# Expert loop: down weights in two places of 4 MB, one kernel before and after

## The chip, the cores and the metric

The kernel runs on one core of one Trainium2 chip. The metric is the device time of one execution in microseconds (us). The core has a matrix engine (TensorE, PE in the profile), a vector engine (VectorE, DVE), a scalar engine (ScalarE, ACT), GpSimd (POOL) and SyncE (SP), which issues all transfers here. Each has its own stream of instructions; they meet at semaphores. On chip there is the SBUF (128 partitions) for operands and the PSUM (8 banks) for products.

## The reference, cut to what matters

A block with attention, a linear recurrence and a mixture of experts comes first, then two layers with attention, pooling and a feed-forward part. Everything is float32, for 256 tokens of width 1024. The change lies in the experts:

```python
logits = (hf @ w_router + b_router)
top_vals, top_idx = lax.top_k(logits, TOP_K)      # 4 of 32 experts for each token
gates = jax.nn.softmax(top_vals, axis=-1)
...
def expert_block(args):                           # xb: the tokens of expert e
    xb, e = args
    gu = xb @ w_gu[e] + b_gu[e]                   # w_gu[e]: 1024 x 2048, 8 MB
    gate = jnp.minimum(gu[:, :D_EXPERT], SWIGLU_LIMIT)
    up = jnp.clip(gu[:, D_EXPERT:], -SWIGLU_LIMIT, SWIGLU_LIMIT)
    glu = gate * jax.nn.sigmoid(SWIGLU_ALPHA * gate)
    return ((up + 1.0) * glu) @ w_down[e] + b_down[e]   # w_down[e]: 1024 x 1024, 4 MB
```

The outputs are weighted by the gates and added up for each token.

## The kernel before, in words

**Stages.** The mixer (attention and recurrence) and the router come first, then the loop over the 32 experts, then the two layers. Expert e is written e0 to e31 below. The weights of the next stage are fetched while the one before computes.

**The ring.** Expert weights go through `ring`, 24576 words (96 KB) in each partition, exactly one expert: eight pieces gu0 to gu7 (1 MB each: 128 rows of w_gu, gate and up) and four pieces dn0 to dn3 (1 MB each: 256 rows of w_down). A piece of expert e+1 goes where the same piece of expert e lay. `load_expert` on SyncE issues one transfer (DMA) for each piece in the order gu0 to gu7, dn0 to dn3. It first waits until TensorE has used the piece that lies there: `gu_used`, or `up_full` for gu7, and `dn_used`, or `y_full` for dn3. SyncE works in order, so a piece that has to wait holds back all behind it. Expert 0's pieces are issued when the mixer has used the ring.

**One expert.** By the count of its tokens an expert takes one round (up to 64 tokens), three (up to 160) or four; `by_count` loads the count into a register and branches to a body written out for that number of rounds, on each of TensorE, ScalarE and VectorE. With this data 30 experts take one round and two take three (their third with 32 slots for each half, called few, L1068 and L1082). A round on TensorE: the bias product (L1072), gate and up with the weights as the moving operand (L1085, 32 matmuls, 64 in the trace since a float32 product runs as two), the combine of the round before (L1051), transposes of the gates (L1103), the gather of the next tokens (L1037), transposes of the hidden values (L1121), transposes of the gathered tokens (L1044), and the down product (L1141, 16 matmuls, 32 in the trace). In between VectorE clips and multiplies (L2086 to L2101) and copies the transposed hidden values (L2104), and ScalarE computes the sigmoid (L1608) and empties banks. A weight piece is given free (`gu_used`, `dn_used`) only in an expert's last round.

**Before the loop.** SyncE sends the gate and up biases to memory and fetches them back transposed (`bias_raw`, L674, "the bias transfers"); ScalarE (L1583) and VectorE (L1977) make `bias_pair` of them and raise `bias_ready`. VectorE adds the mixer's product to x (L1986). The fills of the mixer have names; `o3` is the last attention product, `ad2` the last modulation product, `rt` the transposed router logits.

**Places in the SBUF.** `heap` follows the ring. The mixer's tiles and the experts' small tiles are carved from it, one over the other.

## Time and profile before

| | |
|---|---|
| Time, median of 3 executions | 2127.07 us (2123.1 to 2129.1) |
| The profiled execution's own time | 2125.6 us |
| Its span, from the first to the last instruction | 2123.8 us |
| Mean granted TensorE clock | 0.987 of full speed |
| Gate and up products (L1085) | 492.1 us busy, 2176 matmuls |
| Down products (L1141) | 255.1 us busy, 1152 matmuls |
| Moved by DMA | 580.37 MB, mean 273 GB/s |

The profile shows one execution. An engine's busy time is not its share of the path: a busy engine may be waiting work that something else paces. The loop runs from 186 to 1210 us, 32 us for an expert on average. Which transfers and which products pace it must be read from the waits and from the chain of what released what.

### The profile page before, as it was taken

What the parts mean: (1) busy time and instruction counts of PE and PEld (TensorE: products, weight loads), DVE (VectorE), ACT (ScalarE), POOL (GpSimd) and SP (SyncE); (2) the same over time, 40 slices, a digit from 0 to 9 for tenths busy, and PEclk for the clock granted to TensorE, in tenths of its full rate; (3) what the DMA queues carried; (4) which work ended last, traced back from release to release, by engine and by line L of the source; (5) the groups of instructions that cost most, each with busy time, mean ns of one, the idle gap of its engine ahead of it and who ended that gap; (6) DMA issues with size and microseconds to landing.
All of it is one profiled execution on the core that took longest, in us unless ns stands there. A gap on an engine that the chain in (4) does not pass through costs nothing.

```text
span 2123.8 us, 32004 instructions
## 1 busy us (share of the span) xinstructions
PE 2027.8 (95%) x12406; PEld 1301.0 (61%) x12407; DVE 911.2 (43%) x1611; ACT 645.8 (30%) x981; POOL 59.9 (3%) x65
## 2 busy tenths in 40 slices
PE   6999999999999999999999999999999999999999
PEld 4864333433333333332333498979999899799999
DVE  2522122112222112221112356966786548776774
ACT  1422111101111111110111234564554354644653
POOL 0000000000000000000000022000000120000000
PEclk8997999999999999999999999999999999999999
DMA  9785999299999999999769953423665544234563
GB/s 351 272 329 242 396 417 417 118 417 417 419 418 417 417 419 418 417 417 418 294 250 418 372 153 111 156 72 105 199 214 164 157 132 144 98 120 159 172 196 110
DMA packets 222041, 580.37 MB, mean 273 GB/s; under 512 B 23520, under 2 KB 142048, under 8 KB 185984
## 3 DMA queue, kind: packets, MB, share of 16 engines
q1 hardware_dynamic: 221952, 579.09, 71.6%
q8 instruction: 67, 1.10, 0.2%
q14 instruction: 22, 0.18, 0.0%
HBM read 577.74 MB, written 1.31 MB: 273 GB/s over the span
## 4 chain that ended last, share of the span: by engine, by line
PE 70%; DMA 12%; SPq 9%; DVE 4%; ACT 3%; issue 2%; ACTq 0%; DVEq 0%
PE bank L1085 13%; DMA ring<-in_w_gu 9%; PE bank L1141 8%; SPq L685 4%; SPq L687 4%; PE bank L1226 3%; PE bank L1228 3%; PE bank L1227 3%; PE bank L1457 3%; PE bank L1459 3%; PE bank L1458 3%; PE bank L1037 3%; PE bank L1051 3%; PE bank L812 3%; PE bank L882 2%
## 5 line engine op out<-in xcount | busy, mean ns | idle before, releaser
L1085 PE MATMUL bank<-ring,heap 128*64 128x512 f32 x2176 | 492.1, 601 | 31.7 <-DMA ring<-in_w_gu 31.7
L1085 PEld LDWEIGHTS bank<-ring,heap 128*64 128x64 f32 x2176 | 148.3, 137 | 358.5 <-issue 261.8
L2086 DVE TENSOR_SCALAR heap<-bank 128x256 f32<-128x256 f32 (+1 forms) x72 | 26.7, 413 | 726.2 <-PE bank L1085 697.5
L1141 PE MATMUL bank<-ring,heap 128*64 128x512 f32 (+1 forms) x1152 | 255.1, 595 | 0.0
L1226 PE MATMUL bank<-h_hi,w_hi 128*128 128x256 f32 x640 | 185.2, 289 | 2.2 <-DVE w_lo L2172 1.2
L2367 DVE TENSOR_TENSOR w_lo<-ring,w_hi 128x2048 fp32r<-128x2048 f32 (+1 forms) x64 | 142.4, 2226 | 98.8 <-ACT w_hi L1780 98.8
L1608 ACT ACT_TABLE_LOAD x32 | 41.1, 1283 | 472.5 <-DVE heap L2086 470.8
L1457 PE MATMUL bank<-h_hi,w_hi 128*128 128x256 f32 x640 | 181.7, 284 | 2.4 <-DVE w_lo L2367 2.4
L1227 PE MATMUL bank<-h_lo,w_hi 128*128 128x256 f32 x640 | 182.5, 285 | 0.0
L1228 PE MATMUL bank<-h_hi,w_lo 128*128 128x256 f32 x640 | 182.4, 285 | 0.0
L1458 PE MATMUL bank<-h_lo,w_hi 128*128 128x256 f32 x640 | 181.1, 283 | 0.0
L1459 PE MATMUL bank<-h_hi,w_lo 128*128 128x256 f32 x640 | 181.1, 283 | 0.0
L1141 PEld LDWEIGHTS bank<-ring,heap 128*64 128x64 f32 (+1 forms) x1152 | 78.5, 135 | 150.9 <-issue 145.1
L1780 ACT ACTIVATE w_hi<-ring 128x2048 fp32r<-128x2048 f32 (+1 forms) x64 | 119.2, 1862 | 146.0 <-PE bank L1459 85.5
L2172 DVE TENSOR_TENSOR w_lo<-ring,w_hi 128x2048 fp32r<-128x2048 f32 x52 | 119.3, 2296 | 39.7 <-ACT w_hi L1668 39.7
L1226 PEld LDWEIGHTS bank<-h_hi,w_hi 128*128 128x128 f32 x640 | 124.1, 194 | 5.7 <-DVE w_lo L2172 3.5
L1457 PEld LDWEIGHTS bank<-h_hi,w_hi 128*128 128x128 f32 x640 | 122.8, 192 | 2.8 <-DVE w_lo L2367 2.8
L1227 PEld LDWEIGHTS bank<-h_lo,w_hi 128*128 128x128 f32 x640 | 124.2, 194 | 0.1
L1228 PEld LDWEIGHTS bank<-h_hi,w_lo 128*128 128x128 f32 x640 | 124.2, 194 | 0.0
L1458 PEld LDWEIGHTS bank<-h_lo,w_hi 128*128 128x128 f32 x640 | 122.9, 192 | 0.1
L1459 PEld LDWEIGHTS bank<-h_hi,w_lo 128*128 128x128 f32 x640 | 122.8, 192 | 0.0
L1668 ACT ACTIVATE w_hi<-ring 128x2048 fp32r<-128x2048 f32 x52 | 99.2, 1909 | 72.2 <-PE bank L1228 54.7
(350 smaller groups left out, 2993.7 us busy)
## 6 DMA issues: line engine op xcount, KB each, us to landing
ring<-in_w_gu SPq DMA_DIRECT2D x256, 1024.0 KB, 19.2
ring<-in_w_down SPq DMA_DIRECT2D x128, 1024.0 KB, 22.3
ring<-in_ffn_w_up SPq DMA_DIRECT2D x44, 1024.0 KB, 7.7
ring<-in_w_in SPq DMA_DIRECT2D x32, 1024.0 KB, 8.0
ring<-in_w_ada SPq DMA_DIRECT2D x24, 1024.0 KB, 10.8
ring<-in_ffn_w_down SPq DMA_DIRECT2D x16, 1024.0 KB, 5.4
ring<-in_w_out SPq DMA_DIRECT2D x8, 1024.0 KB, 5.0
ring<-in_w_in SPq DMA_DIRECT2D x3, 2048.0 KB, 26.7
```

The costliest lines, as they stand in the source:

```text
L1085: last = mm(psum[g][both[f], :], xgT[:, k % 4, k // 4, :], wt[:, g, :, :, f, :].rearrange("p i c n -> p (i c) n"), start=False, stop=k == ...
L1141: last = mm(psum[2][FEW * f:FEW * f + n, :], hidT[:, o:o + n], wt[:, 512 * f:512 * (f + 1)], start=k == 0, stop=k == DT - 1)
L1226: mm(out, wh, x[0][:, k, :], start=k == 0, stop=False)
L1227: mm(out, wh, x[1][:, k, :], start=False, stop=False)
L1228: last = mm(out, wl, x[0][:, k, :], start=False, stop=k == nk - 1)
L1457: mm(b[:, g, :], wh, h_hi[:, k, :], start=k == 0, stop=False)
L1458: mm(b[:, g, :], wh, h_lo[:, k, :], start=False, stop=False)
L1459: last = mm(b[:, g, :], wl, h_hi[:, k, :], start=False, stop=k == DT - 1)
L1668: f(hi, src, ACT.Copy).then_inc(S["whi"].sem, 1)
L1780: f(hi, src, ACT.Copy).then_inc(S["whi"].sem, 1)
L2172: v.tensor_tensor(lo, src, hi.bitcast(F32), ALU.subtract).then_inc(S["wlo"].sem, 1)
L2367: v.tensor_tensor(lo, src, hi.bitcast(F32), ALU.subtract).then_inc(S["wlo"].sem, 1)
```

## The change

The down weights get two places of 4 MB, chosen by the parity of the expert: place 0 is where they lay in the ring, place 1 lies in the heap, above the first 4672 words. The transfers of dn for expert e+2 are issued where those of expert e+1 were, after the same waits for expert e; those of expert 1 are issued ahead of the loop, after `rt` and `bias_ready`. The small tiles of the experts move up in the heap, some mixer tiles share space, and `b_down` is loaded after `o3`, ahead of the bias transfers. On TensorE the loop over 32 experts becomes 16 times an inner loop over 2, and the down product is written once for each place, under an If on the parity, in every round of every body.

```diff
@@ -52,6 +52,8 @@
 DN_K = UNIT // T
 SPLIT = 2 * DT * T + 4 * UNIT + 2 * FT * T
 STOP = None
+DOWN_AT = 2 * DT * T + 2 * T + 64
+DOWN_GAP = 8192 + DOWN_AT
 LCH = {"dve": 125, "pool": 23}
 ROUNDS = 4
 CLASSES = ((64, 1), (160, 3), (256, 4))
@@ -266,11 +268,13 @@
 
         with nc.sbuf_tensor("ring", [P, RING], F32) as ring, nc.sbuf_tensor("heap", [P, HEAP], F32) as heap:
             pass
+        with nc.sbuf_tensor("below_down", [P, 16384], F32), nc.sbuf_tensor("down", [P, 2 * DOWN_GAP], F32) as down:
+            pass
         sb("layer_ring", [P, LRING])
         h_hi, h_lo = sb("h_hi", [P, DT, T], F32R), sb("h_lo", [P, DT, T], F32R)
         w_hi, w_lo = sb("w_hi", [P, 2, UNIT], F32R), sb("w_lo", [P, 2, UNIT], F32R)
         f_hi, f_lo = sb("f_hi", [P, FT, T], F32R), sb("f_lo", [P, FT, T], F32R)
-        sb("between", [P, 16384 - LRING])
+        sb("between", [P, HEAP - 2 * (32 + 64 * 4 + 32) - 2 * 512 - 2 * FEW - (SPLIT - (RING - LRING))])
         bias_pair = sb("bias_pair", [P, 2, 512], F32R)
         bias_sel = sb("bias_sel", [P, 2, FEW], F32R)
         psum = [ctx.enter_context(nc.psum_tensor(f"bank{b}", [P, 512], F32))[:, :] for b in range(8)]
@@ -361,6 +365,7 @@
         rstd = take(2, T)
         modT = take(48)
         scale1, scale2 = take(8), take(8)
+        w_route = take(DT, NE)
         qT = take(4, T)
         kT = take(2, T)
         vtok = take(TT, P)
@@ -370,17 +375,14 @@
         lru_a, lru_u = take(4, T), take(4, T)
         lru_t = take(4, T)
         decay, decay2 = take(4), take(4)
-        small_done = take(1)
         mod_rows = take(512)
         w_rg = take(2 * 4, 64)
         small = take(64)
         probs = take(NH, 384)
-        pT = take(2, 384)
+        pT = xg.rearrange("p a b -> p (a b)")[:, 0:2 * 384].rearrange("p (a b) -> p a b", a=2)
         stat = take(8, 2, NH)
         attnT = take(4, T)
-        w_route = take(DT, NE)
-        assert take.areas[0][1] <= 19800, take.areas
-        b_down = heap[0:NE, 19800:19800 + D]
+        assert take.areas[0][1] <= 18752, take.areas
         xn = sq
         merged = sq
         flat_probs = probs.rearrange("p a b -> p (a b)")
@@ -429,13 +431,16 @@
         take_e = Carve()
         take_e.areas[0][1] = 2 * DT * T + 2 * T + 64
 
+        down_two = down.rearrange("p (a b) -> p a b", a=2)
+        take_e(8192)
         x_tok = take_e(512)
         xgT = take_e(4, 2, FEW)
         act_g, act_u, act_s = take_e(512), take_e(512), take_e(512)
         hid, hidT, y_sb = take_e(512), take_e(512), take_e(512)
         sgT = take_e(T)
         pick, pickg = take_e(TT, T), take_e(TT, 2 * T)
-        gateT = take_e(T)
+        gateT = act_g[:, 0:T]
+        b_down = heap[0:NE, take_e.areas[0][1] - 4352:take_e.areas[0][1] - 4352 + D]
         expert_end = take_e.areas[0][1]
         router_at = HEAP - TT * 320
         assert expert_end <= router_at, (expert_end, router_at)
@@ -658,7 +663,6 @@
                 sp.dma_start(mix_piece(name), w_out[:, k:k + 4, :]).then_inc(mix_in[name].sem, 16)
             sp.dma_start(w_route, dram["w_router"].rearrange("(k p) n -> p k n", p=P)).then_inc(route_in.sem, 16)
             sp.dma_start(vec2_all[:, :, :], dram["vec2"]).then_inc(route_in.sem, 16)
-            sp.dma_start(b_down, dram["b_down"]).then_inc(route_in.sem, 16)
             for c in range(DT):
                 last_of("xr1" if c < 2 else "xg1" if c < 4 else "v" if c == 4 else "q1")
                 load_ada(1, c)
@@ -668,13 +672,15 @@
                 else:
                     last_of("ad1")
                 load_ada(2, c)
+            last_of("o3")
+            sp.dma_start(b_down, dram["b_down"]).then_inc(route_in.sem, 16)
             sp.wait_ge(bias_sent.sem, 16)
             sp.wait_ge(merged_ready.sem, 1)
             for g in range(4):
                 sp.dma_start(bias_raw[NE * g:NE * (g + 1)].rearrange("e g (c n) -> e (g c) n", n=P),
                              bias_rows.rearrange("e (b f n) -> f e b n", f=2, n=P)[g % 2]).then_inc(bias_in.sem, 16)
 
-            def load_expert(e, free, names):
+            def load_expert(e, free, names, place=0):
                 gu = dram["w_gu"][e].rearrange("(k p) n -> p k n", p=P)
                 dn = dram["w_down"][e].rearrange("(k p) n -> p k n", p=P)
                 for name in names:
@@ -684,7 +690,8 @@
                     if name.startswith("gu"):
                         sp.dma_start(piece(exp_stream, name, 1)[:, 0, :], gu[:, j, :]).then_inc(exp_in[name].sem, 16)
                     else:
-                        sp.dma_start(piece(exp_stream, name, 2), dn[:, 2 * j:2 * j + 2, :]).then_inc(exp_in[name].sem, 16)
+                        to = down_two[:, place, 2 * D * j:2 * D * (j + 1)].rearrange("p (k n) -> p k n", k=2)
+                        sp.dma_start(to, dn[:, 2 * j:2 * j + 2, :]).then_inc(exp_in[name].sem, 16)
 
             def after_mixer(name):
                 lo = exp_stream.at[name]
@@ -701,8 +708,13 @@
 
             exp_names = [name for name, _ in EXPERT]
             load_expert(0, after_mixer, exp_names[0:4] + exp_names[8:12] + exp_names[4:8])
-            with sp.Fori(0, NE - 1) as e:
-                load_expert(e + 1, after_expert(e), exp_names)
+            last_of("rt")
+            load_expert(1, lambda name: (bias_ready.sem, 1), exp_names[8:], 1)
+            with sp.Fori(0, NE // 2 - 1) as i:
+                for q in range(2):
+                    load_expert(2 * i + q + 1, after_expert(2 * i + q), exp_names[0:8])
+                    load_expert(2 * i + q + 2, after_expert(2 * i + q), exp_names[8:], q)
+            load_expert(NE - 1, after_expert(NE - 2), exp_names[0:8])
             if stop == "moe":
                 sp.wait_ge(xin_ready.sem, 8)
                 sp.dma_start(out.rearrange("(k p) t -> p k t", p=P), xT[:, :, :]).then_inc(out_stored.sem, 16)
@@ -1052,7 +1064,7 @@
                                   skip_group_check=True)
                 return last
 
-            def expert(e, rounds):
+            def expert(e, rounds, q):
 
                 for r, at, u in turns(rounds):
                     final = r == rounds - 1
@@ -1128,21 +1140,28 @@
                     turn_gathered().then_inc(xT_full.sem, u)
 
 
-                    for k in range(DT):
-                        if k % 4 == 0:
-                            pe.wait_ge(hidT_ready.sem, hidT_ready.at(2 * at + (k // 4 + 1) * u, e))
-                        if r == 0 and k % 2 == 0:
-                            pe.wait_ge(exp_in[f"dn{k // 2}"].sem, exp_in[f"dn{k // 2}"].at(16, e))
-                        wt = piece(exp_stream, f"dn{k // 2}", 2)[:, k % 2, :]
-                        h, c, f = k // 4, k // 2 % 2, k % 2
-                        o = P * h + FEW * f + FEWER * c if few else P * (2 * h + c) + FEW * f
-                        n = FEWER if few else FEW
-                        for f in range(2):
-                            last = mm(psum[2][FEW * f:FEW * f + n, :], hidT[:, o:o + n], wt[:, 512 * f:512 * (f + 1)],
-                                      start=k == 0, stop=k == DT - 1)
-                        if final and k % 2 and k < DT - 1:
-                            last.then_inc(dn_used.sem, 1)
-                    last.then_inc(y_full.sem, u)
+                    def down_products(place):
+
+                        for k in range(DT):
+                            if k % 4 == 0:
+                                pe.wait_ge(hidT_ready.sem, hidT_ready.at(2 * at + (k // 4 + 1) * u, e))
+                            if r == 0 and k % 2 == 0:
+                                pe.wait_ge(exp_in[f"dn{k // 2}"].sem, exp_in[f"dn{k // 2}"].at(16, e))
+                            wt = down_two[:, place, D * k:D * (k + 1)]
+                            h, c, f = k // 4, k // 2 % 2, k % 2
+                            o = P * h + FEW * f + FEWER * c if few else P * (2 * h + c) + FEW * f
+                            n = FEWER if few else FEW
+                            for f in range(2):
+                                last = mm(psum[2][FEW * f:FEW * f + n, :], hidT[:, o:o + n], wt[:, 512 * f:512 * (f + 1)],
+                                          start=k == 0, stop=k == DT - 1)
+                            if final and k % 2 and k < DT - 1:
+                                last.then_inc(dn_used.sem, 1)
+                        last.then_inc(y_full.sem, u)
+
+                    with pe.If(q <= 0):
+                        down_products(0)
+                    with pe.Else():
+                        down_products(1)
 
             drained_mix("ht3")
             pe.wait_ge(pick_ready.sem, 1)
@@ -1162,8 +1181,9 @@
                    skip_group_check=True)
             pe.wait_ge(slots_ready.sem, 2)
             pe.wait_ge(bias_ready.sem, 1)
-            with pe.Fori(0, NE) as e:
-                by_count(pe, e, expert)
+            with pe.Fori(0, NE // 2) as i:
+                with pe.Fori(0, 2) as q:
+                    by_count(pe, 2 * i + q, lambda e, rounds: expert(e, rounds, q))
             pe.wait_ge(y_ready.sem, y_ready.at(R, NE))
             combine().then_inc(combined.sem, R)
             pe.wait_ge(xT_ready.sem, xT_ready.at(R, NE))
@@ -2069,7 +2089,7 @@
             select_bias(0).then_inc(sel_ready.sem, 1)
             dve.wait_ge(gate_ready.sem, 1)
             select_gates(0).then_inc(pickg_ready.sem, 1)
-            v.tensor_copy(small_done, gsum[:, 0, 0:1]).then_inc(slots_ready.sem, 1)
+            v.tensor_copy(rstd[:, 1, 0:1], gsum[:, 0, 0:1]).then_inc(slots_ready.sem, 1)
 
             def expert(e, rounds):
                 for r, at, u in turns(rounds):
```

## Rows read from the trace of the kernel before

**Rows 1.** The page: an engine's busy time, GB/s in 40 slices of the span, DMA issues.

```profile
PE 2027.8 (95%) x12406; PEld 1301.0 (61%) x12407; DVE 911.2 (43%) x1611; ACT 645.8 (30%) x981; POOL 59.9 (3%) x65
GB/s 351 272 329 242 396 417 417 118 417 417 419 418 417 417 419 418 417 417 418 294 250 418 372 153 111 156 72 105 199 214 164 157 132 144 98 120 159 172 196 110
...
ring<-in_w_gu SPq DMA_DIRECT2D x256, 1024.0 KB, 19.2
```

**Rows 2.** The chain that ended last: start us, us, what.

```profile
301.70 13.88 PE bank L1085 x64
...
328.90 13.88 PE bank L1085 x64
...
651.45 25.06 DMA ring<-in_w_gu
...
711.70 25.05 DMA ring<-in_w_gu
```

**Rows 3.** Windows: busy time of PE, PEld, DVE, ACT, POOL; clock, DMA share, GB/s.

```profile
170.00:187.00 17.00, 14.36 (x34) 7.64 (x36) 4.91 (x20) 1.64 (x4) 0.00 (x0) 0.54 0.01 1
375.50:411.50 36.00, 35.80 (x201) 13.35 (x204) 4.50 (x12) 4.12 (x8) 0.00 (x0) 1.00 0.01 1
...
366.00:383.00 17.00, 16.80 (x88) 6.62 (x84) 3.98 (x10) 2.69 (x6) 0.00 (x0) 1.00 0.56 223
...
660.00:720.00 60.00, 55.38 (x266) 19.23 (x264) 12.32 (x36) 8.38 (x14) 0.00 (x0) 1.00 1.02 418
```

**Rows 4.** SyncE's timeline, 340 to 480.

```profile
411.83 6.35 SPq L685 DMA_DIRECT2D ring<-in_w_gu  x8
```

**Rows 5.** Timeline, TensorE: e6's first gate and up, e27's last eight.

```profile
356.04 13.95 PE L1085 MATMUL bank<-ring,heap 128*64 128x512 f32 x64
...
1037.99 1.94 PE L1085 MATMUL bank<-ring,heap 128*64 128x512 f32 x8 [0.55 <-DMA ring<-in_w_gu]
```

**Rows 6.** The longest waits from 436 to 1026: total, times, longest.

```profile
PEld bank L1085 <- DMA ring<-in_w_gu: 88.6, 74, 1.5
...
PE bank L1085 <- DMA ring<-in_w_gu: 29.6, 58, 0.6
```

**Rows 7.** Timeline before the loop, 85 to 170.

```profile
116.35 6.77 SPq L674 DMA_DIRECT2D heap<-bias_rows  x4
...
127.66 0.38 PE L949 MATMUL bank<-heap 128*64 128x128 f32 x2
...
137.67 1.05 ACT L1583 ACTIVATE bias_pair<-heap 128x1024 fp32r<-128x1024 f32 x1
...
138.75 1.22 DVE L1977 TENSOR_TENSOR bias_pair<-heap,bias_pair 64x1024 fp32r<-64x1024 f32 x1 [2.52 <-ACT bias_pair L1583]
...
151.60 0.88 DVE L1986 SCALAR_TENSOR_TENSOR xT<-bank,heap,xT 128x256 f32<-128x256 f32 x2 [2.58 <-PE bank L927]
...
166.17 0.23 DVE L2015 TENSOR_TENSOR heap<-bank,vec 128x64 f32<-128x64 f32 x1 [5.08 <-PE bank L1012]
```

**Rows 8.** ScalarE's timeline, 1200 to 1245.

```profile
1224.31 3.70 ACT L1668 ACTIVATE w_hi<-ring 128x2048 fp32r<-128x2048 f32 x2
```

**Rows 9.** Timeline, the middle and end of a round of e2.

```profile
265.81 0.76 DVE L2104 COPY heap<-bank 128x256 f32<-128x256 f32 x2 [1.25 <-PE bank L1121]
...
266.18 0.63 PE L1044 MATMUL bank<-consts_sb,heap 128*128 128x128 f32 x4 [0.26 <-ACT heap L1616]
...
266.74 7.09 PE L1141 MATMUL bank<-ring,heap 128*64 128x512 f32 x32
...
273.76 0.73 PE L1072 MATMUL bank<-bias_pair,bias_sel 128*128 128x512 f32 x2
```

**Rows 10.** The chain after e0 and after e6.

```profile
213.84 3.82 issue
...
430.28 3.92 issue
```

**Rows 11.** DMA from 205 to 220: packets, MB, share.

```profile
q8 instruction: 3, 0.05, 1.3%
```

## The prediction

> **What bounds the kernel now.** I read the page first: the engine table, the slices, the queues and the costliest groups. TensorE (PE) is busy 95% of the span, and in most slices of the expert loop (the 5th to the 19th) DMA moves 417 to 419 GB/s [rows 1]. Both look full, so the page alone can't say which of them sets the loop. The chain of waits can. In one kind of stretch it runs through TensorE only, and an expert takes 328.90 - 301.70 = 27.2 us [rows 2]: 13.88 for gate and up (L1085), 7.02 for down (L1141), the rest for the small products between. In the other kind each link holds 25 us of a w_gu transfer, and two experts take 711.70 - 651.45 = 60.25 us [rows 2], 30.13 each. That is the transfer of one expert: 12 pieces of 1024 KB [rows 1], 12.58 MB, at 418 GB/s [rows 3] are 30.1 us. So DMA is the slower supplier by 2.9 us per expert, and TensorE is the bound only while a stock lasts.
>
> The windows and SyncE's timeline tell how the stock comes and goes. Loading rests from 170 to 187 us and from 375.5 to 411.5 (DMA share 0.01 in both) [rows 3]. The second rest begins at 366 + 0.56 x 17 = 375.5 and ends when L685 issues again at 411.83 [rows 4]. A third, like the second, lies at 1046 to 1082. The last two belong to the experts with three rounds, e6 (its first round starts at 356.04) and e27 (its first gate and up end at 1037.99 + 1.94 = 1039.9) [rows 5]: a gu piece comes free only in the last round, so SyncE waits at gu0 of the next expert. Three streams result. The first starts at about 187.5 and ends at 375.5: gu1 dn1 ... gu6 dn6, and TensorE sets the pace. The second starts at 411.83: 21 times gu and 20 times dn up to the end of gu27, (21 x 8.39 + 20 x 4.19) MB / 0.418 = 622 us, landing at about 1036. The last eight matmuls of gate and up in e27's first round start at 1037.99 and wait for DMA until then [rows 5], so this stream pins that place, whatever TensorE does between. From there TensorE sets the pace again to the end of the loop.
>
> The next question is which piece is late. The list of waits from 436 to 1026 has 88.6 us of weight loads and 29.6 us of matmuls waiting for in_w_gu, and no wait for in_w_down [rows 6]. Down weights are never late, in no stretch.
>
> **The change, part by part.** (a) The second place lets dn of expert e+2 start where dn of e+1 started: SyncE waits for the same counts in the same order (gu_used of e, then dn_used of e), and only the expert whose dn moves is another. In the second stream 21 gu and 20 dn precede the end of gu27 as before, now dn8 to dn27 instead of dn7 to dn26. The bytes ahead of every gu piece are the same, the rest from 375.5 to 411.8 stays (SyncE stands at gu0 of e7), and the stream pins the same place. What becomes early is what was never late: 0 us.
>
> (b) Those 4.19 MB are paid once, ahead of the loop. They go out after rt and bias_ready. Rt is full when VectorE takes it at 166.17, bias_ready comes with L1977 at 138.75 + 1.22 = 140.0 [rows 7]. Expert 0's loads end at about 170, so dn1 runs from 170 to 180 in a rest that lasts to 187.5: 0 us. If it were later, the first stream has a stock: dn6 is the last 10 us before 375.5, so gu6 is there at 365.5, and TensorE wants its eighth piece at 356.04 + 7/8 x 13.95 = 368.2 [rows 5]. The first 2.7 us of a delay would be lost there.
>
> (c) b_down now leaves after o3 and stands before the bias transfers, which L1583 on ScalarE waits for. o3's matmuls end at 127.66 + 0.38 = 128.0; the bias transfers, issued in 6.77 us from 116.35, are issued from some 128.5 and take 6.8 at most, to 135. Today they land at the latest 137.67 - 123.12 = 14.5 us of the last issue, behind loads of w_ada that are done by then. Counting from 135, landing lies between 137 and 149.5 (those 14.5 us once more, in full), and L1583 with it. Behind it on ScalarE are the squares of x1, on VectorE L1977 and the four L1986 that feed ss2. The last of these runs at 151.60 because TensorE's product ends there, and bias split, two memsets and three such steps take 1.22 + 3 x 0.88 = 3.9 us and some 0.5 for the small ones [rows 7]. VectorE may start at 151.6 - 4.4 = 147.2, ScalarE 1.05 earlier, at 146.1. 0 us; at the upper end of the landing 149.5 - 146.1 = 3.4, and as nothing but the bias transfers is in the engines then, the low end is the nearer.
>
> (d) The last stream loses one dn ahead of the next layer's loads, 10 us earlier. TensorE starts the layer straight behind L1175, and ScalarE's first split of a weight (L1668, at 1224.31) shows no wait for DMA [rows 8]. 0 us.
>
> (e) TensorE's new If stands in each round between the last transposes (L1044) and down. Nothing in the trace is such a branch with no matmuls queued. The branches at an expert's end lie behind 7 us of queued down products and cost nothing: L1141 starts at 266.74 and runs 7.09, and the next expert's L1072 starts at 273.76 with no gap [rows 9]. In the middle the queue is short: L1044 starts at 266.18, hidT's copy (L2104) ends at 265.81 + 0.76 = 266.57, L1141 starts 0.17 later. Lower bound 0, if the branch is decided while the sequencer would wait for L2104 anyway. A step of TensorE's sequencer is priced by the 0.17 between a release and the start, wait included; upper bound two such, 0.34. I take 0.14, nearer the lower, since the time up to L2104's end is about what L1044's own instructions take. Which rounds show it: e0 to e5, and two rounds of e6 (8), then three of e27 and e28 to e31 (7). The other 21 rounds lie under the second stream. 15 x 0.14 = 2.1 us (0 to 5.1). If the cover of the stream were gone, 36 x 0.14 = 5.0. The Trainium skill (Advanced Engine Details and Errata, Control Flow Timing) gives 108 ns for compare-and-branch and 51 ns for a plain branch; by it this term would be an estimated 15 x 0.16 = 2.4 us, and no run here shows a branch alone.
>
> (f) The inner loop adds a few register steps at an expert's end, behind the same 7 us: 0.
>
> (g) Code. TensorE idles 3.82 us before the second expert and 3.92 us after e6 [rows 10], and three 16 KB packets of instructions (q8) travel from 205 to 220 [rows 11]; an answer for 301 to 356 has no such line, nor have those from 440 to 1215. So code once fetched stays, also for both bodies: no packet travels around e27, the second expert with three rounds. The down product doubled adds 16 matmuls (64 instructions with their halves and weight loads) per round to three bodies, so e27 may find something thrown out: 0, or 3.9 once. I take 0.
>
> **Sum.** 2.1 us on 2125.6, the profiled execution's own time (its span, 2123.8, and 1.8 around it). That execution is 1.5 under the median of 2127.07, inside the 6 us between the lowest and highest run. On the median: 2129.2, I say 2129. 0.3%, what a measurement here tells from no change, is 6.4 us.
>
> **Rivals.** *The stock grows* (faster). If the 4.19 MB were to travel in the rest before 411.83 and each gu came earlier by them, the second stream would be 10.0 us shorter, 2127.1 - 10 + 2.1 = 2119. For it: a rest of 36 us is there, and DMA sets 15 experts. Against: SyncE's order. It decides whether anything moves between 376 and 411. Chance 0.08, with all smaller gains of the kind.
>
> *The branch is dear* (slower). It decides from 6.4 / 15 = 0.43 us per round, over two of the 0.17 steps: a compare, a jump and recomputed wait values that nothing overlaps. At 0.5 us: 15 x 0.5 = 7.5, 2134.6; with one code stall more 2138.5. Nothing excludes it. Chance 0.12.
>
> *Each expert fetches code* (slower). With 3.85 us in each exposed round, 15 x 3.85 = 58 us; and from e7, which starts at 430.28 + 3.92 + 1.2 = 435.4, an expert would take 27.2 + 3.85 = 31.05, more than DMA's 30.13. Gate and up of e27 would end at 435.4 + 20 x 31.05 + 13.9 = 1070.3 instead of 1039.9, 30 us later, 88 in all: 2215. Against: bodies that jump over 3- and 4-round code run without a single instruction packet. The Trainium skill (Runtime: NRT & Kernel Launch, Instruction fetch mechanics) says that a taken branch to a target outside the current two-page window stalls on a fetch; by that rule each expert's exit would stall today, and the trace disagrees from the third expert on. Chance 0.02.
>
> *The early dn1 pushes gu1* (slower). It decides when dn1 starts after 177.5 + 2.7 = 180.2; at the worst, all 10 us behind 187.5, it costs 10 - 2.7 = 7.3 and 2.1: 2136.5. (10 us are 4.19 MB at 418 GB/s.) Rt at 166 speaks against it. With the bias transfers late as in (c) 0.03.
>
> **How the numbers follow.** The forecast, unchanged but for 0 to 6 us of control flow, has the remaining 0.75. Its own bounds: 2127.07 - 3 (how far the medians of such executions may differ, half of the spread shown) to + 5.1 + 3.9: 2124 to 2136, with (c) at its worst 2139. The range 2122 to 2137 reaches partway to the faster rival and holds the cheap end of the dear branch, leaving out a little under 2 in 10. Faster 0.08; slower 0.12 + 0.02 + 0.03 = 0.17; same 0.75.
>
> **What would show it.** (a) The rest before the second stream still ends some 36 us after it begins, the waits for in_w_gu still total about 118 us between e7 and e27, a little less for a longer middle, and none for in_w_down. (b) A w_down issue at 166 and busy DMA from 170 to 180. (c) L1583 before 146. (e) The 27.2 us period grows to 27.3 or 27.4, two experts under the stream stay at 60.25. (g) instruction packets around e27. I would be wrong if the second stream is shorter, if the middle grows by over 0.4 us, or if the first experts wait for gu.

## The result, and the profile after

The changed kernel takes 2143.8 us (median of 5 runs, 2138.9 to 2146.4), the kernel before in the same rounds 2124.9 (5 runs, 2121.2 to 2129.1). The ratio is 1.0086 [1.0074, 1.0098]: 0.9% slower, 18.9 us. The forecast was 2129 with a range up to 2137. The profiled executions span 2144.3 and 2123.8 us.

The page of the kernel after: TensorE's row, GB/s in 40 slices, and the queue that brings instructions (packets, MB, share).

```profile
PE 2029.2 (95%) x12406; PEld 1304.3 (61%) x12407; DVE 911.3 (42%) x1611; ACT 644.3 (30%) x981; POOL 59.8 (3%) x65
GB/s 353 262 339 317 416 417 405 136 374 417 419 418 417 417 418 419 418 417 417 247 260 418 276 115 113 183 63 118 197 196 178 145 127 154 99 118 151 170 201 109
q8 instruction: 80, 1.31, 0.3%
```

TensorE works nearly as long as before [rows 1]: 1.4 us more. The lost time is idle time. The page of the kernel before has 67 packets of instructions, this one 80: 1.31 MB, 16 KB each. The chain says where the idle time is (start us, us, what):

```profile
214.42 3.25 issue
218.39 13.88 PE bank L1097 x64
...
245.59 13.88 PE bank L1097 x64
...
272.79 13.88 PE bank L1097 x64
...
428.56 11.53 issue
441.31 15.75 PE bank L1097 x64
...
685.73 25.09 DMA ring<-in_w_gu
...
745.98 25.08 DMA ring<-in_w_gu
...
1104.44 11.63 issue
1117.29 15.68 PE bank L1097 x64
```

L1097 is gate and up (L1085 before), L1155 down (L1141), L1084 the bias product (L1072). "issue" is time in which TensorE waits for nothing that the profile shows. Before there were two such stretches, 3.82 us after e0 and 3.92 after e6 [rows 10]. Now there are three: 3.25, 11.53 after e6, and 11.63 after e27, where before there was none. The list of waits puts all of them on the first matmuls of an expert (total, times, longest):

```profile
PE bank L1084 <- issue: 26.4, 3, 11.6
```

The packets of instructions are at the same places: from 1100 to 1125 us the DMA view of the kernel after shows four (the line below), nine from 1000 to 1215, and in the kernel before there is none from 450 to 1215. In windows of 1 us the four travel at 1104, 1110 (two, the second line below) and 1117 us; around the wait after e6 they travel at 428, 434 (two) and 441. So the first packet comes within 1 us of the wait's start, two come together 6 to 7 us later, and the last comes when TensorE already runs again. The 3.92 us after e6 in the kernel before have one packet at 430 and one, behind the wait, at 436.

```profile
q8 instruction: 4, 0.07, 1.5%
```
```profile
q8 instruction: 2, 0.03, 24.6%
```

How much of each stall counts is told by the starts of single pieces. The 7.6 us more after e6 end in the second stream, which has some slack. In two windows (busy PE, PEld, DVE, ACT, POOL; clock, DMA share, GB/s) the kernel after reads:

```profile
405.00:428.00 23.00, 22.52 (x224) 9.84 (x218) 4.84 (x18) 2.68 (x6) 0.00 (x0) 1.00 0.73 299
428.00:450.00 22.00, 10.47 (x38) 3.29 (x36) 0.00 (x0) 0.60 (x1) 0.00 (x0) 0.69 0.83 324
```

and the kernel before:

```profile
405.00:428.00 23.00, 22.52 (x224) 9.98 (x220) 4.83 (x18) 2.69 (x6) 0.00 (x0) 1.00 0.65 266
428.00:450.00 22.00, 18.08 (x78) 5.64 (x74) 0.36 (x2) 0.60 (x1) 0.00 (x0) 0.92 1.02 415
```

The stream restarts 1.7 us earlier (L691 issues at 410.11, before 411.83 [rows 4]), since in this execution e1's gate and up take 13.88 us, and in that of the kernel before 15.58. But TensorE stands still until 440, no gu piece comes free, and SyncE, which had issued dn8 from 423.61, issues the next gu only at 445.11. The stream runs dry: 22 x (415 - 324) is 2.0 MB less, 4.8 us of it, of which the earlier restart had gained 1.8 (23 x (299 - 266) is 0.76 MB). The last eight matmuls of e27's first gate and up start at 1042.22 and not 1037.99 [rows 5]: 4.2 us late, of which these two windows explain 3.0. The 4.2 is one pair of executions: this start lies between 1035.5 and 1038.0 in the nine kernels here with the old order on SyncE and no long wait, and between 1037.5 and 1044.6 in the seven with two long waits. The 11.63 us after e27 have no cover at all, and the idle engine's clock goes down with it. After e6 the mean granted clock is 0.69 in the second window, before 0.92: part of it is at the lower of the clock's two levels, 1.2 GHz. After e27 it is 0.62 while TensorE idles and 0.88 behind that, where the kernel before has 1.00:

```profile
1104.00:1117.00 13.00, 1.37 (x6) 0.50 (x2) 0.00 (x0) 0.60 (x1) 0.00 (x0) 0.62 1.02 402
1117.00:1133.00 16.00, 16.00 (x67) 5.00 (x66) 0.76 (x2) 0.26 (x1) 0.00 (x0) 0.88 0.75 299
```

So e28's bias product takes 1.21 us and not 0.66, its gate and up 15.68 and not 13.88. Its gate and up start at 1117.29, before at 1100.87: 16.4 late. The last expert hands over to the layers (L1270) at 1237.99, before 1220.04: 17.95 late. In sum: 4.2 + 11.6 + 0.6 + 1.8 = 18.2, of which 0.3 is made up again before the layers. The spans differ by 20.5 us and the medians by 18.9; the profiled execution of the kernel after is the slowest of its five. The layers take 906.3 us of the span, before 903.8, on which more at the end.

### The profile page after: what moved, and what is told of

Same layout as the page of the kernel before. It is cut to its first block, busy times and chain, and to the rows that moved or that the text cites. A ratio compares the mean times of both kernels' runs of the same rounds, so it can differ in the third digit from the quotient of the medians.

```text
span 2144.3 us, 32040 instructions
## 1 busy us (share of the span) xinstructions
PE 2029.2 (95%) x12406; PEld 1304.3 (61%) x12407; DVE 911.3 (42%) x1611; ACT 644.3 (30%) x981; POOL 59.8 (3%) x65
## 3 DMA queue, kind: packets, MB, share of 16 engines
q8 instruction: 80, 1.31, 0.3%
HBM read 577.74 MB, written 1.31 MB: 270 GB/s over the span
## 4 chain that ended last, share of the span: by engine, by line
PE 71%; DMA 12%; SPq 8%; DVE 4%; ACT 3%; issue 3%; ACTq 0%; DVEq 0%
PE bank L1097 13%; DMA ring<-in_w_gu 9%; PE bank L1155 8%; SPq L691 4%; PE bank L1246 3%; PE bank L1248 3%; PE bank L1247 3%; SPq L694 3%; PE bank L1477 3%; PE bank L1478 3%; PE bank L1479 3%; PE bank L1049 3%; PE bank L1063 3%; PE bank L824 3%; PE bank L894 2%
## 5 line engine op out<-in xcount | busy, mean ns | idle before, releaser
L1097 PE MATMUL bank<-ring,heap 128*64 128x512 f32 x2176 | 492.3, 601 | 30.0 <-DMA ring<-in_w_gu 30.0
L1097 PEld LDWEIGHTS bank<-ring,heap 128*64 128x64 f32 x2176 | 148.9, 138 | 356.7 <-issue 266.1
L1155 PE MATMUL bank<-down,heap 128*64 128x512 f32 (+1 forms) x1152 | 255.1, 595 | 0.0
L1155 PEld LDWEIGHTS bank<-down,heap 128*64 128x64 f32 (+1 forms) x1152 | 78.6, 135 | 150.8 <-issue 145.0
```

Of the source, the lines that this page charges most:

```text
L1097: last = mm(psum[g][both[f], :], xgT[:, k % 4, k // 4, :], wt[:, g, :, :, f, :].rearrange("p i c n -> p (i c) n"), start=False, stop=k == ...
L1155: last = mm(psum[2][FEW * f:FEW * f + n, :], hidT[:, o:o + n], wt[:, 512 * f:512 * (f + 1)], start=k == 0, stop=k == DT - 1)
```

## The experiments

The theory after this reading: TensorE keeps only part of its instructions on chip; the loop with its doubled products no longer fits, and after each three-round expert it has to fetch code again, three blocks in series of some 3.9 us each. (The packets above don't bear out the three equal steps: of the three that travel before TensorE runs again, two travel together. How the 11.6 us split into fetches stays open.) The rival causes are the branch and the nested loop as executed, and the two places themselves. I counted positions in the compiled programs, in instructions of 64 bytes from the start of TensorE's program; 256 of them are a packet of 16 KB, here a block. These positions come from the programs and stand in no trace.

**Code alone, loop alone.** e1_code_only is the kernel before with the new loop and both copies of the down products, both reading the old place. e2_nest_only has the new loop alone.

```diff
-            with pe.Fori(0, NE) as e:
-                by_count(pe, e, expert)
+            with pe.Fori(0, NE // 2) as i:
+                with pe.Fori(0, 2) as q:
+                    by_count(pe, 2 * i + q, expert)
```

> The kernel before with TensorE's part of the change alone: nested loops, the down product written twice under the If, but both copies read the old place; all transfers and tiles are those of before. Theory 'code' (the doubled products make the loop's code too large to stay on chip, so that after each expert with three rounds TensorE waits for three fetches in a row): idle of 11.5 us after e6 and again after e27, about 80 q8 packets, ratio to before 1.008 to 1.010. Rival 'data' (the second place, the early dn1 or the moved tiles disturb the transfers): idle of 3.9 and 0 us, 67 packets, ratio 0.999 to 1.001. Rival 'branch' (the If costs in every round): the 27.2 us period of an expert grows by at least 0.4 us.

> The kernel before with TensorE's loop nested (16 times 2) and nothing else: no If, one down product. Theory 'code': the loop is a few instructions longer, idle of 3.9 us after e6 and 0 to 3.9 after e27 (the last instructions of the outer loop now cross into the next 256), ratio 0.999 to 1.003. Rival 'nesting' (a loop in a loop costs at its back edge): idle of 11 us at both places, ratio 1.008 to 1.010.

e1_code_only: ratio 1.0093 [1.0075, 1.0112], with waits of 3.48, 10.87 and 11.02 us at 211, 429 and 1103 us. e2_nest_only: 0.9993 [0.9982, 1.0005]. So the whole loss comes with TensorE's code, and within the intervals none of it with the data, the tiles or the nesting.

**Less code that nobody runs, and another order of it.** No expert of this data takes four rounds. e4_no_body4 is the changed kernel without those bodies (`CLASSES = ((64, 1), (160, 3))`); e5_long_first writes them ahead of the others.

> The changed kernel without the bodies for four rounds on all three engines (more than 160 tokens, which no expert of this data has). Every instruction that runs is the same; the loop's end now lies right behind the three-round body. Theory 'code, counted by the blocks that are touched': 7 blocks of 256 instead of 9, idle of at most 3.9 us after e6 and 0 after e27, ratio to before 0.998 to 1.001. If instead the If or the two places cost by themselves: idle of 11.5 us as in the changed kernel, ratio 1.008 to 1.010.

> The changed kernel whole, with the body for four rounds written first instead of last on each engine, so that the bodies for one and three rounds and the loop's end lie together (8 blocks of 256 touched instead of 9 or 10). Theory 'code by touched blocks': idle of 3.9 us or less after e6 and 0 to 3.9 after e27, one new fetch at the first expert at most, ratio to before 0.999 to 1.004. If a fetch is due to each far jump whatever is touched: head and body lie far apart now, and idle of 8 to 12 us after e6 and e27 stays, ratio 1.008 or more.

e4_no_body4: 0.9998 [0.9988, 1.0009], the waits of 11 us are gone, though both copies and the If on the parity still run as in the changed kernel; only e6 and e27 have one test of the count less. e5_long_first: 1.015 [1.0111, 1.0189]; its chain has

```profile
211.84 12.14 issue
253.01 3.97 issue
443.02 11.63 issue
1118.38 10.12 issue
```

This is a miss: the theory wanted at most 1.004, and the rival, a fetch at each far jump, wanted 1.008 or more. That rival falls later, with e7_copy_in_four (the exits jump further, no cost) and e13_shifted (they jump as far as before, full cost). So the branch costs nothing, and where the executed code lies does.

**The complete kernel, four-round body put elsewhere; copies only where nobody goes.** e8_far_body4 moves the blocks of that body behind the rest of TensorE's program. e7_copy_in_four is e1_code_only with the copies in that body alone:

```diff
-                    with pe.If(q <= 0):
-                        down_products()
-                    with pe.Else():
-                        down_products()
+                    if rounds == 4:
+                        with pe.If(q <= 0):
+                            down_products()
+                        with pe.Else():
+                            down_products()
+                    else:
+                        down_products()
```

> The changed kernel, complete, down weights in their two places and drawn by parity; only the order of TensorE's instructions is another: the body for four rounds, which no expert of this data takes, stands behind all the rest of TensorE's program and not between the body for three rounds and the end of the loop. No instruction is added or left out on the way that the experts take. Theory (what the loop touches of TensorE's instructions no longer stays loaded, so that blocks of it are fetched again after each three-round expert): the loop with its two short bodies lies together again, as in the kernel without four-round bodies, so one wait for instructions of about 3.3 us at 214 us and none of over 2 us behind it, some 67 packets of instructions, ratio to the kernel before 1.000 (0.998 to 1.002), 19 us under the changed kernel. Rival (it is the branch and the second copy of the products as they are run that cost, or the two places themselves): ratio 1.009 as with the code alone, and the waits of 11.5 us at 429 and 1104 us stay.

> The kernel before with the loop over the experts as two nested ones, and the branch with two equal copies of the down products (both read the one old place) in the body for four rounds alone, which no expert of this data takes. The bodies that run are as before; the loop is some 280 instructions longer, and its end stands 1.1 blocks of 256 instructions later (at 17.1, before 16.0). Theory (the blocks that are touched decide, not how far apart they lie): ratio 1.000 (0.998 to 1.002), waits for instructions of 3.9 us at 430 us and none at 1104 us, some 67 packets. Rival (it is the length of the loop, from its head to its end, that decides): waits of 11.5 us at 429 and 1104 us, some 80 packets, ratio 1.009. A ratio between, with one wait of 3.9 us more, would say that the place of the loop's end in its block matters.

e8_far_body4: 1.0011 [1.0001, 1.0022], one wait of 3.95 us. e7_copy_in_four: 0.9997 [0.9986, 1.0007], waits of 3.59 and 3.85 us as before. The loop may be longer by a whole block here if nobody walks through the longer part.

**How much more is too much.** e10_copy_in_one and e11_copy_in_three have the copies in the one-round and in the three-round body alone (`rounds == 1`, `rounds == 3` above).

> The kernel before with the nested loop, and the branch with two equal copies of the down products (both read the old place) in the body for one round alone: some 70 instructions more; the body for three rounds is as before, but ends two instructions behind the start of the next block of 256 (at 12.00, before 11.73), the loop at 16.25. Theory (it counts how many blocks a three-round expert touches, the next one that is fetched ahead too: one more than before): waits for instructions of 11 us at 429 and 1102 us, some 80 packets, ratio 1.008 to 1.010, for 70 instructions as for the 560 of the change. Rival (the cost grows with the instructions added): an eighth of it, ratio 1.001.

> The same with the branch and the two copies in the body for three rounds alone: some 210 instructions more; that body ends at 12.54, the loop at 16.79; the one-round experts run what they ran before. Theory (number of blocks touched): as many blocks as in the changed kernel, waits of 11 us at 429 and 1102 us, some 80 packets, ratio 1.008 to 1.010. Rival (in proportion to the instructions): three eighths, ratio 1.003.

e10_copy_in_one: 1.0084 [1.0068, 1.01]; e11_copy_in_three: 1.0105 [1.0089, 1.012]. Some seventy instructions cost what the whole change with its 560 does: a step and not a cost in proportion. The chain of e10_copy_in_one:

```profile
211.62 3.64 issue
...
429.11 10.19 issue
...
1102.32 10.54 issue
```

**The loop untouched, its place moved.** In e13_shifted 58 instructions stand ahead of the loop. By my count of blocks this was to bring time.

```diff
+            for _ in range(116):
+                pe.wait_ge(bias_ready.sem, 1)
             with pe.Fori(0, NE) as e:
```

> The kernel before with 58 instructions more on TensorE directly ahead of the loop over the experts (waits for a signal that has long come, two to an instruction), and nothing else: no instruction of the loop is changed, the loop only stands 58 instructions later, so that its head lies at 7.02 blocks of 256 (before 6.81), the end of the body for three rounds at 11.95 (11.73) and the loop's end at 16.2 (15.97). A one- or three-round expert then lies in five blocks and not six. Theory (what counts is the number of blocks touched, and before sat one under the number at which all is fetched again, with one wait of 3.9 us left behind the first three-round expert of the loop proper): no wait for instructions over 2 us behind 214 us, 2 to 4 us under before: ratio 0.998 to 0.999. Rival (the wait of 3.9 us at 430 us is that of the first way past the loop's end, and the place of the code in its blocks has no part in it): that wait stays, ratio 1.000 or a little above.

It was 1.01 [1.0083, 1.0118], waits of 10.81 and 10.24 us at 432 and 1107: slower by as much as the change, with no instruction of the loop altered. Both theories as I had put them fall. If blocks count, as the other runs suggest, their borders can't lie at multiples of 256 of my count. Four more runs moved the loop, by a branch that is never taken:

```diff
+            n = pe.value_load(counts_i[0:1, 0:1], min_val=0, max_val=T)
+            with pe.If(n > T - 1):
+                for _ in range(498):
+                    pe.wait_ge(bias_ready.sem, 1)
             with pe.Fori(0, NE) as e:
```

> The kernel before with its loop 256 instructions later on TensorE: ahead of the loop stands a branch that is never taken, whose body holds the instructions. The loop itself is unchanged. Theory (blocks of 256 instructions, eight of them held; their borders lie somewhere between 3001 and 3023 of my count, and every 256 from there): a shift by a whole block leaves the loop as it was, waits for instructions of 3.9 us at 430 us and none at 1100 us, 67 or 68 packets, ratio 1.000 (0.998 to 1.002). Rival (any longer way to the loop, or what stands ahead of it, costs): waits of 10 to 11 us at 430 and 1103 us, ratio 1.010 as with the loop 58 instructions later.

> The kernel before with its loop 22 instructions later on TensorE, again by a branch that is never taken. The loop itself is unchanged. Theory: before, the loop from its head to the end of the body for three rounds (1258 instructions, five blocks of 256 being 1280) fitted five blocks by luck, which only 22 or 23 of 256 places allow; 22 later it touches six, with the block of the loop's end and the one behind each nine: waits for instructions of 10 to 11 us at 430 and 1103 us, some 80 packets, ratio 1.008 to 1.011. Rival (no such edge, it needs a larger shift, or it was the 58 executed instructions): ratio 1.000, waits as before.

> The kernel before with its loop 128 instructions later on TensorE, by a branch that is never taken. Theory (what counts is how many blocks of 256 the loop touches together with the code fetched ahead; a border lies at the end of the body for three rounds when it stands 23 to 58 later): here that body reaches well past the border, while the loop's head is in the first of these blocks only from some 75 later on at the earliest, so it is open by the runs so far: repeated fetches, waits of 10 to 11 us at 430 and 1103 us and ratio 1.010, if the code fetched ahead reaches far (I hold this likelier, 2 in 3); none, ratio 1.000, if it reaches some tens of instructions.

> The same, 200 instructions later. If the loop 128 later is free of repeated fetches, this one is too: ratio 1.000. If it is not, this one is the last third of the stretch, as likely free as not; free here and not at 128 would say that the costly stretch lies between 23 and at most 199, costly at both that more than half of all places cost 1%.

Against before: 256 later 1.0 [0.9991, 1.0009], waits 3.21 and 3.85 us; 22 later 0.9998 [0.9989, 1.0007], waits 3.31 and 3.59; 128 later 1.0108 [1.0079, 1.0138]; 200 later 1.01 [1.0071, 1.0129], these two from two executions each. The chain with the loop 128 later:

```profile
214.71 3.09 issue
...
428.72 10.68 issue
...
1104.08 10.95 issue
```

The place 22 later was a miss, the one at 256 a hit: 58, 128 and 200 later cost, 0, 22 and 256 are free. If the places between the costly ones are costly too, that is over half of every 256, and the kernel before stood by luck in a favourable one; the places from 23 to 57 and from 201 to 255 were not tried.

**The four-round body far away, in the kernel before.** e18_before_far does nothing else; e17_far_58 has the loop 58 later as well.

> The kernel before with its loop 58 instructions later (by a branch that is never taken) and the body for four rounds behind all the rest of TensorE's program. Theory: the place that cost 1.0% costs nothing here, since the end of the loop follows right behind the body for three rounds: six blocks and the one behind them, seven of eight. No wait for instructions over 2 us behind 215 us, ratio 0.997 to 1.001. Rival (the place of the loop costs by itself): ratio 1.010.

> The kernel before, complete, with nothing but the body for four rounds moved behind all the rest of TensorE's program. Theory: the wait of 3.9 us for instructions at 430 us goes, and with it 2 to 4 us of the time: ratio 0.998 to 0.999, the least change that beats the kernel before. Rival (the wait at 430 us is hidden by the stream behind it, which alone sets the last stream's begin): ratio 1.000.

e17_far_58: 1.0005 [0.9996, 1.0015], one wait of 3.19 us: the costly place costs nothing when the four-round body is out of the loop. e18_before_far: 1.0015 [1.0005, 1.0025]. The wait at 430 us is gone as expected, and the expected 2 to 4 us don't come: its rival is right, the second stream covers 3.9 us (e27's last eight matmuls start at 1036.13, before at 1037.99, a difference that other kernels show with the wait in place, such as e7_copy_in_four with 1036.27). That it is slower at all is the layers' part (below).

**What the two places can bring.** In the changed kernel SyncE's order keeps the stock unused. e6_by_count_no_body4 (without four-round bodies) and e9_far_by_count (complete) let SyncE read the count of expert e; TensorE then waits for all four down transfers of an expert at once:

```diff
+            def load_next(e, place):
+                n = sp.value_load(counts_i[0:1, bass.ds(e, 1)], min_val=0, max_val=T)
+                with sp.If(n <= CLASSES[0][0]):
+                    load_expert(e + 1, after_expert(e), exp_names[0:8])
+                    load_expert(e + 1, after_expert(e - 1), exp_names[8:], place)
+                with sp.Else():
+                    load_expert(e + 1, after_expert(e - 1), exp_names[8:], place)
+                    load_expert(e + 1, after_expert(e), exp_names[0:8])
```

> The changed kernel with no body for four rounds on any engine (no expert of this data takes one), so without the waits for instructions, and with the stock really drawn: SyncE reads the number of tokens of expert e, and where it takes three rounds it issues the down weights of e+1 ahead of the gate/up weights of e+1, so that they travel while TensorE is in the first rounds and the DMA rests; where it takes one round it issues gate/up of e+1 first and the down weights of e+1 behind. The down weights of e+1 wait for e-1 only. Theory: the down weights (4.2 MB, some 10 us of the stream) that before travel behind the gate/up weights after a three-round expert now travel in its rest, so each of the two streams behind a three-round expert starts with 10 us in stock; one of them shows in the end, the other may be lost in the rest that follows: 2105 to 2118 us, ratio 0.991 to 0.997. Rival (the rest is full, or the stock is lost because SyncE's queue stands still in another order and TensorE then waits for the down weights at one-round experts): ratio 1.000 or above, with waits of TensorE for the down weights in the list of waits.

> A complete kernel: the changed one with the body for four rounds behind all the rest of TensorE's program, and with SyncE issuing the down weights of expert e+1 ahead of its gate/up weights where expert e takes more than one round, behind them where it takes one. Theory: no wait for instructions of over 4 us, and the stock drawn: within 2 us of the same kernel without four-round bodies, ratio 0.991 to 0.997, faster than both kernels. Rival (the body put far away costs more elsewhere on TensorE's program, in the layers that stand between): several waits of 3 to 4 us more than without four-round bodies, ratio 1.000 or above.

e6_by_count_no_body4: 2120.07 us, 0.9982 [0.9972, 0.9991]. e9_far_by_count: 2123.46 us, 0.9999 [0.9989, 1.0009]. Both miss the expected 0.991 to 0.997. The chain of e8_far_body4, the same complete kernel with the old order, at the end of the second stream:

```profile
1011.68 26.27 DMA ring<-in_w_gu
1037.99 1.94 PE bank L1097 x8
...
1045.51 7.02 PE bank L1155 x32
```

and of e9_far_by_count:

```profile
1009.85 27.42 DMA down<-in_w_down
1037.32 7.09 PE bank L1166 x32
```

The stream isn't shorter: its last piece lands at 1037.95 in the one and at 1037.27 in the other, and as many bytes lie ahead of it. But now it is dn27 and not gu27, and what TensorE does between the two (1.94 us and the middle of the round) is over when it comes: down starts 8.2 us earlier. That is the gain, and not the 10 us that the 4.19 MB take at 418 GB/s. In the first stream, where TensorE sets the pace, there is none: from 217.76 to 429.58 us, where e7 starts, e9_far_by_count takes 211.8 us, e8_far_body4 from 218.28 to 430.83 takes 212.6, and the latter has 1.7 more in e1's gate and up (15.58 against 13.88), which the order of the transfers doesn't explain. In e6_by_count_no_body4 the DMA even idles for part of the time from 200 to 220 us (share 0.57), as the down weights stand behind gate/up pieces whose places are taken:

```profile
200.00:220.00 20.00, 17.61 (x83) 6.16 (x84) 3.90 (x13) 2.18 (x4) 0.00 (x0) 1.00 0.57 231
```

e12_far_drawn tries the other order: the down weights of an expert with several rounds, and no others, are held back behind its gate/up weights.

> A complete kernel: the changed one with the body for four rounds behind all the rest of TensorE's program, and the stock drawn at another place than in the last two runs. SyncE always issues the gate/up weights of e+1 first and then, as in the changed kernel, the down weights of e+2, but not where e+2 takes more than one round: those are issued one step later, behind the gate/up weights of e+2, so that they travel while e+2 is in its first rounds. TensorE waits for the four down transfers of an expert at once. Theory: each of the two three-round experts behind the first starts 10 us earlier (4.2 MB at 419 GB/s no longer stand ahead of its gate/up weights), its rest is 10 us fuller, and the DMA never idles at the restart as it did (210 to 220 us) where the down weights were ordered behind the next gate/up ones: the layers start near 1202 us (before 1220), 2105 to 2112 us, ratio 0.991 to 0.994. Rival (only what lies behind the last stream counts, or the gain of the first is lost in the second rest): one of the two shows, 10 us, ratio 0.995 to 0.998. Rival (the first round of the long expert now waits for its down weights at the stream's pace): the down products of its first round start late, with a wait of 5 us or more for the down weights, and less than 5 us in all are left.

1.0005 [0.9996, 1.0014]: the theory and the first rival, both at 0.998 or below, are out. The last rival's "less than 5 us in all are left" fits, but not its reason: TensorE's list of waits has none for the down weights. Its chain:

```profile
980.75 25.11 DMA ring<-in_w_gu
1005.90 1.94 PE bank L1114 x8
...
1021.16 13.88 PE bank L1114 x64
```

gu26 still ends e26's gate and up at 1007.8, so TensorE comes to e27 at 1021.16. There it never waits, and gate and up end at 1035.0, where e8_far_body4 ends them at 1037.99 + 1.94 = 1039.9. The 4.19 MB that no longer stand ahead of gu27 are an estimated 10 us at 418 GB/s, and TensorE can use 4.9. A stock drawn at the last moment meets an engine that is itself not there yet.

Fourteen of the twenty kernels side by side. "Wait 3" is the wait for instructions after e27, "layers from" the start of the first layer's first product in the chain; the last column is the rest of the span.

| kernel | wait 2, wait 3 (us) | layers from | rest |
|---|---|---|---|
| before | 3.92, none | 1220.04 | 903.8 |
| after | 11.53, 11.63 | 1237.99 | 906.3 |
| e1_code_only | 10.87, 11.02 | 1235.76 | 906.4 |
| e10_copy_in_one | 10.19, 10.54 | 1235.43 | 904.5 |
| e13_shifted | 10.81, 10.24 | 1239.36 | 906.2 |
| e7_copy_in_four | 3.85, none | 1218.01 | 903.5 |
| e16_unrun_22 | 3.59, none | 1217.22 | 906.2 |
| e17_far_58 | none | 1218.55 | 906.0 |
| e4_no_body4 | none | 1217.87 | 909.2 |
| e8_far_body4 | none | 1219.90 | 909.1 |
| e18_before_far | none | 1218.75 | 908.8 |
| e9_far_by_count | none | 1211.61 | 910.4 |
| e12_far_drawn | none | 1215.06 | 910.6 |
| e6_by_count_no_body4 | none | 1209.73 | 908.7 |

## Why the prediction was wrong

**(g) Code, the step that failed.** I read that no packet of instructions travels around e27, concluded that "code once fetched stays, also for both bodies", and took 0 for 64 instructions more per round, 3.9 us once at the worst. The observation was right, the conclusion was not: the loop of before stood at a place where its code just stays, and that row can't tell a store with room from one that is full. Going over the edge doesn't cost one fetch in proportion to what was added, but the reload of blocks of the loop around each three-round expert, nine packets around e27 where there was none: 7.6 us more of waiting after e6 and 11.6 after e27, of which 17.95 us reach the layers, the low clock included. e1_code_only (all of it), e4_no_body4 and e8_far_body4 (none of it), e10_copy_in_one (all of it for 70 instructions) and e13_shifted (all of it for a move) show this. The rival "each expert fetches code" had the right mechanism at the wrong frequency, one-round experts among themselves fetch next to nothing (one packet from 450 to 1000 us), and my numbers for it, 88 us, made it look remote. The case between the two, each long expert fetches code, should have been priced: 2 experts x 3 fetches x 3.85 us less the 3.92 already there, 19 us. That this sum comes so near is in part luck: the packets show no three equal steps, and the second stream covers part of the first wait.

**(a) The stream pins its end, whatever TensorE does.** Right about the order of bytes: nothing moved up, the rest before the second stream stays, there is still no wait for in_w_down, and two experts under the stream take 745.98 - 685.73 = 60.25 us as before. Wrong in "whatever TensorE does": SyncE needs the places that TensorE gives free. One stall of 3.9 us at the stream's start is covered (e18_before_far), one of 11.5 costs 4.2 in the profiled execution.

**(b) dn1 in the first rest.** Right. It is issued at 166.65, and from 170 to 187 us the DMA moves 3.9 MB where it moved nothing [rows 3]:

```profile
170.00:187.00 17.00, 13.88 (x34) 7.65 (x36) 4.92 (x20) 2.10 (x6) 0.00 (x0) 0.56 0.58 229
```

**(c) Biases.** Right, at the low end of its bounds: the transfers are issued from 128.81, as said, and ScalarE's L1603 starts at 137.95, 0.28 us later than before [rows 7] and far from the 146 at which it would count.

```profile
128.81 2.61 SPq L680 DMA_DIRECT2D heap<-bias_rows  x4
...
137.95 1.05 ACT L1603 ACTIVATE bias_pair<-heap 128x1024 fp32r<-128x1024 f32 x1
```

**(d) The last stream.** Right, 0 us. There is no wait for DMA at the first layer's start; it starts as soon as L1195, the last product of the loop's end, is through at 1237.99, as before.

**(e) The branch.** Taken at 0.14 us in 15 rounds, 2.1 us; it is 0, the one term of the sum that was not nothing. The period is 272.79 - 245.59 = 27.20 us as before. In the middle of e2 hidT's copy ends at 264.11 + 0.76 = 264.87, and the down product starts 0.17 us later, behind the branch as it did without one [rows 9]:

```profile
264.11 0.76 DVE L2124 COPY heap<-bank 128x256 f32<-128x256 f32 x2 [1.25 <-PE bank L1133]
```
```profile
264.49 0.63 PE L1056 MATMUL bank<-consts_sb,heap 128*128 128x128 f32 x4 [0.26 <-ACT heap L1636]
265.04 7.09 PE L1155 MATMUL bank<-down,heap 128*64 128x512 f32 x32
```

So the lower bound held: the branch is decided before the copy ends. The Trainium skill's 108 and 51 ns for a compare-and-branch and a plain branch (Advanced Engine Details and Errata, Control Flow Timing) may be right, but no part of them shows here.

**(f) The inner loop.** 0 as said (e2_nest_only). The rivals of a dear branch and of an early dn1 that pushes gu1 are out; that the stock grows would have needed another order on SyncE, as the argument against it said.

## What to carry to other kernels

A loop whose bodies are picked by data has a size on TensorE, and being free of instruction packets says nothing about the room left. Before adding code to such a loop, compare placements, since here a shift of the untouched loop by 58 instructions cost as much as the change. Bodies that are rarely taken belong behind the loop and not between the taken ones and its end; that took the loss from 1.0086 to 1.0011 without leaving anything out. And a second buffer brings nothing while the queue's order is the same; with the order changed by the count it was worth 8.2 us where the stream sets the pace, by letting the piece come last that is needed last, and nothing where TensorE does. The only kernel here that measures below the one before clear of noise, 0.9982, leaves the four-round bodies out; the complete one is at 0.9999.

## What the runs showed of the hardware

TensorE's instructions are fetched in packets of 16 KB (80 of them are 1.31 MB), and a loop whose exits jump over the bodies for three and four rounds can run for hundreds of microseconds without one (450 to 1215 in the kernel before), so more than the current and the next block is kept. The Trainium skill (Runtime: NRT & Kernel Launch, Instruction fetch mechanics) gives TensorE 2048 instructions of memory, refilled first in, first out in blocks of 256, which would be eight blocks; it also speaks of two lines and of a fetch at each taken branch that leaves the two-page window. The traces speak against the two; the eight they allow and don't show. By my count a store of eight blocks, with a border near instruction 3020 and the block behind each executed stretch fetched too, agrees with all placements: 8 blocks at the most for the free kernels, 9 or more for all that refetch. That is a fit made after the runs, with positions that no trace holds. It is also a tight one: only 22 or 23 places in 256 are free by it, and both 0 and 22 later are free, so the border has hardly more than one instruction of play. Other borders with seven or nine blocks fit as well. So the number held is not shown, only that the cost depends on the place, is absent again 256 later, and comes in one step.

The wait before the second expert takes 2.1 to 4.0 us over the kernels (e5_long_first has a long one there), the long waits 10.1 to 12.1.

Open is a smaller effect of the same kind or another: the layers take 908.7 to 910.6 us in six kernels, all without a four-round body inside the loop, and 903.5 to 906.7 in the other fourteen, e17_far_58 among them although its body is moved too. In e18_before_far a transfer of ffn_w_up stands in the chain with more time than the 7.93 us of before:

```profile
1487.37 9.23 DMA ring<-in_ffn_w_up
```

The longer layers are why e9_far_by_count reaches the layers 8.4 us earlier than before and ends only 1.8 earlier in the span. Whether the cause is where the layers' code lies or where their transfers meet was not tried. It also blurs the small ratios: e8_far_body4's 1.0011 and e18_before_far's 1.0015 come from kernels whose layers take 909.1 and 908.8 us in the profiled executions.
